# A causal pooling mixer for a prompt: band before weights, or weights before band

## What is computed

```python
u = rmsnorm(h, norm_mix[0])
for g, w in enumerate((2, 4, 8, 16)):          # 4 groups of 512 columns
    s = cs[:, P + 1:P + 1 + T, sl] - cs[:, P + 1 - w:P + 1 - w + T, sl]   # window sums of u
    cnt = jnp.minimum(pos + 1, w)
    outs.append(s / cnt)
d = pooled - u
y = einsum('btgc,gcd->btgd', d, w_group) * scale   # one 512x512 matrix per group
h = h + y
h = h + sq_relu_mlp(rmsnorm(h, norm_ffn[0]), w_up[0], w_down[0])
```

## Time and profile before

| | us |
|---|---|
| median of 3 runs | 2453.6 (2453.4 to 2454.82) |
| profiled execution, its own time | 2453.96 |
| its span, first to last instruction | 2452.2 |
| TensorE busy | 2438.4 |
| VectorE busy | 1193.2 |
| ScalarE busy | 908.8 |
| GpSimd busy | 484.9 |
| mean granted TensorE clock | 0.999 |

### The profile page before, as it was taken

The page is one execution under the profiler, slowest core; times in us unless marked ns, Lnnn a source line. Parts: engine busy times, 40 slices in busy tenths (PEclk is TensorE's granted clock), DMA queues, the critical chain, the costliest instruction groups (busy, mean ns, idle before and its releaser), DMA issues.

```text
span 2452.2 us, 43354 instructions
## 1 busy us (share of the span) xinstructions
PE 2438.4 (99%) x16326; PEld 2397.8 (98%) x16326; DVE 1193.2 (49%) x1353; ACT 908.8 (37%) x1080; POOL 484.9 (20%) x616
## 2 busy tenths in 40 slices
PE   9999999999999999999999999999999999999998
PEld 9999999999999999999888899999999999999997
DVE  6644344344444454544578885544344444434444
ACT  6332333333323333323456553332233333323332
POOL 7620022012102332210011112230022013101331
PEclk9999999999999999999999999999999999999999
DMA  6544454454444444555477764444444445445443
GB/s 234 172 151 152 147 153 147 149 150 147 152 146 145 154 147 140 150 142 154 143 249 234 233 202 153 146 146 154 147 153 147 150 143 152 153 146 151 149 147 116
DMA packets 198473, 389.05 MB, mean 159 GB/s; under 512 B 12277, under 2 KB 12533, under 8 KB 197929
## 3 DMA queue, kind: packets, MB, share of 16 engines
q1 hardware_dynamic: 197664, 385.78, 50.2%
q0 software_dynamic: 736, 2.27, 0.3%
HBM read 365.81 MB, written 22.65 MB: 158 GB/s over the span
## 4 chain that ended last, share of the span: by engine, by line
PE 96%; DVE 2%; DMA 1%; ACT 0%; issue 0%; SPq 0%; DVEq 0%; ACTq 0%
PE G L1662 30%; PE G L1664 30%; PE G L1663 30%; PE X L1936 1%; DMA gain<-in_mix_rows 1%; PE X L1899 1%; PE X L1943 0%; DVE cst L1573 0%; DMA w_raw<-in_pool_w 0%; PE G L1975 0%; PE G L1979 0%; PE G L1977 0%; PE X L1834 0%; PE X L1888 0%; DVE w_lo L1170 0%; PE X L1648 0%
## 5 line engine op out<-in xcount | busy, mean ns | idle before, releaser
L1170 DVE TENSOR_TENSOR w_lo<-w_raw,w_hi 128x1024 fp32r<-128x1024 f32 x648 | 826.5, 1277 | 1164.6 <-ACT w_hi L840 1161.1
L840 ACT ACTIVATE w_hi<-w_raw 128x1024 fp32r<-128x1024 f32 x608 | 644.6, 1061 | 1303.9 <-PE G L1664 1275.5
L1662 PE MATMUL G<-op_hi,w_hi 128*128 128x320 f32 x2816 | 875.7, 311 | 0.0
L1664 PE MATMUL G<-op_hi,w_lo 128*128 128x320 f32 x2816 | 871.0, 309 | 0.0
L1663 PE MATMUL G<-op_lo,w_hi 128*128 128x320 f32 x2816 | 870.9, 309 | 0.0
L1662 PE MATMUL G<-a_hi,w_hi 128*128 128x320 f32 x2304 | 714.5, 310 | 1.5 <-DVE hT L1289 0.8
L1663 PE MATMUL G<-a_lo,w_hi 128*128 128x320 f32 x2304 | 713.6, 310 | 0.0
L1664 PE MATMUL G<-a_hi,w_lo 128*128 128x320 f32 x2304 | 713.5, 310 | 0.0
L1662 PEld LDWEIGHTS G<-op_hi,w_hi 128*128 128x128 f32 x2816 | 528.9, 188 | 3.6 <-issue 1.6
L1663 PEld LDWEIGHTS G<-op_lo,w_hi 128*128 128x128 f32 x2816 | 529.0, 188 | 2.6 <-issue 1.0
L1664 PEld LDWEIGHTS G<-op_hi,w_lo 128*128 128x128 f32 x2816 | 528.9, 188 | 0.0
(11 more groups left out here) (282 smaller groups left out, 1015.0 us busy)
## 6 DMA issues: line engine op xcount, KB each, us to landing
w_raw<-in_ffn_w_up SPq DMA_DIRECT2D x256, 512.0 KB, 3.7
w_raw<-in_ffn_w_down SPq DMA_DIRECT2D x256, 512.0 KB, 3.7
w_raw<-in_mlstm_w_in SPq DMA_DIRECT2D x96, 512.0 KB, 3.9
w_raw<-in_mlstm_w_out SPq DMA_DIRECT2D x32, 512.0 KB, 4.5
cst<-in_state_mlstm_C SPq DMA_DIRECT2D x24, 512.0 KB, 3.9
out_C_sample<-cst SPq DMA_DIRECT2D x24, 512.0 KB, 3.2
w_raw<-in_pool_w SPq DMA_DIRECT2D x8, 512.0 KB, 11.4
w_raw<-in_state_mlstm_C SPq DMA_DIRECT2D x8, 512.0 KB, 4.2
```

The source lines that it names most:

```text
L840: act.activation(w_hi[:, c % RING], w_raw[:, c % RING], ACT.Copy).then_inc(w_hi_ok, 1)
L1170: v.tensor_tensor(w_lo[:, slot], w_raw[:, slot], w_hi[:, slot].bitcast(F32), ALU.subtract).then_inc(w_lo_ok, 1)
L1662: pe.matmul(G[:, m, 0:T], w_hi[:, slot, t, w], hi[:, k, :], start=first and t == 0, stop=False)
L1664: ins = pe.matmul(G[:, m, 0:T], w_lo[:, slot, t, w], hi[:, k, :], start=False, stop=last and t == CK - 1)
```

## The change

The order of the two products is turned round for the prompt. The group's weights are applied first, to the unnormed columns of x times the gains, with x as the stationary operand and 512 weight columns moving, so that the result is token-major; then the band, with the roots in it, mixes the tokens of the result and turns it feature-major. In detail:

- SyncE loads vectors, hT's first quarter and two weight chunks first; the sample rows and a slice of gains next; the prompt's rows later. Gains come in three pieces, and the last of them, hT's last quarter and the kept far inputs stand behind the load of chunk 5.
- ScalarE and VectorE split hT times the gain into a_hi and a_lo (`xt_hi`, `xt_lo`), without roots.
- The samples keep their order, band first: their sums go to G's fourth bank and are split into one operand of 64 hi and 64 lo columns (`pairs`), for which two products do for three. That gives hi and lo parts of y on 128 rows; `fold` adds them.
- y is copied out of PSUM: first prompt tile and samples by ScalarE (`y_first`, `y_samples`), second prompt tile by VectorE (`y_second`).
- TensorE mixes a group after the next group's weight products (`mix`); the last group's mixing stands behind the first chunk of the first FFN slab.
- Warm-up is 9 + 20 products in one piece. GpSimd draws fold ahead of the bands of groups 1 to 3, and all draws before any scaling. The squares of the sample tile come first.

```diff
-WARM = (13, 5, 8, 6)
+WARM = 20
+ROW_ORDER = (2, 0, 1)
...
+            sp.dma_start(vecs[:, :], A["vec_cols"]).then_inc(vecs_in, 16)
+            residual_load(0)
+            pool_load(0)
+            pool_load(1)
+            rows_load(2)
+            gain_load(0)
+            residual_load(1)
+            pool_load(2)
+            gain_load(1)
+            pool_load(3)
+            rows_load(0)
+            rows_load(1)
+            residual_load(2)
...
             for n in range(RING, 2 * GROUPS):
                 sp.wait_ge(w_lo_ok, n - RING + 1)
                 pool_load(n)
+                if n == RING + 1:
+                    gain_load(2)
+                    residual_load(3)
+                    sp.dma_start(far[0:NS, :], A["state_far"]).then_inc(far_in, 16)
...
             draw(0)
+            link(pool.memset(fold[:, :], 0.0))
+            for at in (0, NS):
+                pool.affine_select(out=fold[:, :], in_=fold[:, :], compare_op=ALU.not_equal, fill=1.0, base=-at,
+                                   pattern=[[-1, NS]], channel_multiplier=1).then_inc(fold_ok, 1)
+                pool.wait_ge(fold_ok, 2 if at else 1)
             for g in range(1, GROUPS):
                 draw(g)
+            for g in range(1, GROUPS):
                 rooted(g)
...
+            def xt_hi(k):
+                act.wait_ge(h_in[k // MT], 16)
+                act.activation(a_hi[:, k, 0:TP], hT[:, k, 0:TP], ACT.Copy, scale=vec(V_MIX + k)).then_inc(xt_hi_ok, 1)
+            def pair_hi(g):
+                act.wait_ge(s_sum, g + 1)
+                if g > 1:
+                    act.wait_ge(gemm, pool_used(g - 2, 1))
+                act.activation(pairs[:, g % 2, :, 0:NS], sample_part(G[:, 3]), ACT.Copy).then_inc(s_hi_ok, 1)
+            def y_first(g):
+                act.wait_ge(gemm, pool_tile(g, 0))
+                if g > 1:
+                    act.wait_ge(mixed, MT * (g - 1))
+                act.activation(ytok[:, g % 2, 0, :], G[:, 0, :], ACT.Copy).then_inc(y_act, 1)
...
+            for g in range(2, GROUPS):
+                xt_hi(MT * g)
+                xt_hi(MT * g + 1)
+                y_first(g - 1)
+                split_pool(2 * g)
+                xt_hi(MT * g + 2)
+                xt_hi(MT * g + 3)
+                y_samples(g - 1)
+                split_pool(2 * g + 1)
+                pair_hi(g)
+                op_his(g - 2)
+                squares_of(g - 2)
+            split(0, 0)
+            y_first(GROUPS - 1)
+            split(0, 1)
+            y_samples(GROUPS - 1)
+            op_his(GROUPS - 2)
+            squares_of(GROUPS - 2)
+            split(0, LEAD - 1)
+            op_his(GROUPS - 1)
+            squares_of(GROUPS - 1)
...
+            xt_lo(4)
+            xt_lo(5)
+            pair_lo(0)
+            split_pool(2)
+            y_second(0)
+            xt_lo(6)
+            xt_lo(7)
+            samples(1)
+            split_pool(3)
+            pair_lo(1)
             v.wait_ge(band_drawn, 1)
             half_square(1)
             tile_inverse(1)
+            rooted(0)
             half_square(2)
             tile_inverse(2)
+            rooted(1)
+            for g in range(2, GROUPS):
                 v.wait_ge(h_in[g], 16)
+                xt_lo(MT * g)
+                xt_lo(MT * g + 1)
+                split_pool(2 * g)
+                y_second(g - 1)
+                xt_lo(MT * g + 2)
+                xt_lo(MT * g + 3)
+                samples(g)
+                pooled(g - 2)
                 split_pool(2 * g + 1)
+                pair_lo(g)
...
+            def pool_rows(g, c, t):
+                at = (2 * g + c) % RING
+                for i in range(CK):
+                    k, first, last = 2 * c + i, c == 0 and i == 0, c == 1 and i == 1
+                    if t == 2:
+                        pe.matmul(G[:, t, :], pairs[:, g % 2, k, :], w_hi[:, at, i, :], start=first, stop=False, skip_group_check=True)
+                        ins = pe.matmul(G[:, t, :], pairs[:, g % 2, k, :], w_lo[:, at, i, :], start=False, stop=last, skip_group_check=True)
                     else:
+                        hi, lo = a_hi[:, MT * g + k, tok(t)], a_lo[:, MT * g + k, tok(t)]
+                        pe.matmul(G[:, t, :], hi, w_hi[:, at, i, :], start=first, stop=False, skip_group_check=True)
+                        pe.matmul(G[:, t, :], lo, w_hi[:, at, i, :], start=False, stop=False, skip_group_check=True)
+                        ins = pe.matmul(G[:, t, :], hi, w_lo[:, at, i, :], start=False, stop=last, skip_group_check=True)
+            def mix(g):
+                pe.wait_ge(y_act, 2 * g + 2)
+                pe.wait_ge(y_dve, g + 1)
+                pe.wait_ge(fold_ok, 2)
+                if g:
+                    pe.wait_ge(band_ok, 2 * g)
+                else:
+                    pe.wait_ge(band0_ok, 2)
+                for m in range(MT):
+                    if g:
+                        pe.wait_ge(evicted, MT * (g - 1) + m + 1)
+                    own = slice(m * P, (m + 1) * P)
+                    pe.matmul(X[m][:, 0:BT], ytok[:, g % 2, 0, own], band[:, g, B0:B1], start=True, stop=False, skip_group_check=True)
+                    pe.matmul(X[m][:, P:TP], ytok[:, g % 2, 1, own], band[:, g, B1:BS], start=False, stop=True, skip_group_check=True)
+                    pe.matmul(X[m][:, TP:T], ysam[:, g % 2, own], fold[:, :], start=False, stop=True, skip_group_check=True).then_inc(mixed, 1)
+            keep_warm(WARM)
+            for c in range(2):
+                pe.wait_ge(xt_lo_ok, 2 * c + 2)
+                pe.wait_ge(w_lo_ok, c + 1)
+                ins = pool_rows(0, c, 0)
+                if c:
+                    ins.then_inc(gemm, 1)
+                    samples(0)
+                pool_rows(0, c, 1).then_inc(gemm, 1)
+            pe.wait_ge(s_lo_ok, 1)
+            pool_rows(0, 0, 2)
+            pool_rows(0, 1, 2).then_inc(gemm, 1)
+            for g in range(1, GROUPS):
+                samples(g)
                 for c in range(2):
+                    pe.wait_ge(xt_lo_ok, MT * g + 2 * c + 2)
+                    pe.wait_ge(w_lo_ok, 2 * g + c + 1)
+                    for t in range(TT):
+                        if c == 0 and t == 1:
+                            pe.wait_ge(y_dve, g)
+                        elif c == 0:
+                            pe.wait_ge(y_act, 2 * g if t else 2 * g - 1)
+                        if t == 2:
+                            pe.wait_ge(s_lo_ok, g + 1)
+                        ins = pool_rows(g, c, t)
+                        if c or t == 2:
+                            ins.then_inc(gemm, 1)
+                mix(g - 1)
...
-                slab(s0, op_hi, op_lo, op_ready(j_op), lambda c: norm_sum(j_op) if c == 4 else None)
+                slab(s0, op_hi, op_lo, op_ready(j_op),
+                     lambda c: norm_sum(j_op) if c == 4 else mix(GROUPS - 1) if c == 0 and s0 == S_FFN0 else None)
```

More of the change, by code:

```diff
@@ L677, in _ @@
                 select(seqmask[at:at + NS, 2, 1:], [[TS, NSEQ]], -1, base=TS - 1)
-            link(pool.memset(fold[:, :], 0.0))
-            for at in (0, NS):
-                select(fold[:, :], [[-1, NS]], 1, base=-at, op=ALU.not_equal, fill=1.0)
             with nc.allow_non_contiguous_dma("a few values"):
@@ L911, in _ @@
+            act.wait_ge(vecs_in, 16)
+            xt_hi(0)
+            xt_hi(1)
+            split_pool(0)
+            xt_hi(2)
+            xt_hi(3)
+            split_pool(1)
             square(0)
             tile_root(0)
+            xt_hi(4)
+            xt_hi(5)
+            pair_hi(0)
+            split_pool(2)
+            y_first(0)
+            xt_hi(6)
+            xt_hi(7)
+            split_pool(3)
+            y_samples(0)
+            pair_hi(1)
             square(1)
@@ L1290, in pooled @@
                                            op0=ALU.mult, op1=ALU.add).then_inc(evicted, 1)
[L1292 to L1303 removed]
+            v.wait_ge(consts, 1)
@@ L1304, in _ @@
+            op_split(0, 0, V_FFN)
+            split(0, 0)
             op_split(0, 1, V_FFN)
-            pooled(GROUPS - 1)
+            y_second(GROUPS - 1)
+            split(0, 1)
             op_split(0, 2, V_FFN)
             op_split(0, 3, V_FFN)
-            split(0, 1)
+            pooled(GROUPS - 2)
+            op_split(0, 4, V_FFN)
+            op_split(0, 5, V_FFN)
+            pooled(GROUPS - 1)
             split(0, LEAD - 1)
-            for k in (4, 5):
-                op_split(0, k, V_FFN)
@@ L1701, in samples @@
+                pe.wait_ge(u_ok, g + 1)
+                if g:
+                    pe.wait_ge(s_lo_ok, g)
+                if g == GROUPS - 1:
+                    pe.wait_ge(far_in, 16)
                 for i in range(MT):
-                    at = slice(TP + i * NS, TP + (i + 1) * NS)
-                    ins = pe.matmul(X[0][:, at], xrow[0:rows, 2, features(g, i)], band[0:rows, g, BS:BP], start=False,
```

(32 more changed lines are left out.)

249 lines of the change are left out of this document (107 added, 142 removed).

## The result

The changed kernel takes 2461.73 us (median of 7; 2460.15 to 2464.11) against 2453.4 of the kernel before beside it: ratio 1.0034, 95% interval 1.0024 to 1.0043, slower by 8.3 us. The forecast was 2456.5, with a range of 2452 to 2461. The profiled execution took 2463.59, with a span of 2461.8 against 2452.2.

What follows compares the result with a forecast made beforehand. TensorE's instruction stream was taken to bound the kernel. The old median 2453.6, plus 1.3 us for a later second FFN chunk and 1.6 for a low-clock spell, gave 2456.5 us, range 2452 to 2461.

Steps and rivals of the forecast that it cites:

- the third wait of TensorE: Idle ahead of the last group's sample products, samples(3), at 44.2 us; put at 0.2 us.
- the clock: One spell at the lower level of 1.2 GHz near 47 to 50 us, costing 1.6 us as before.
- the work behind the mark: TensorE's stream after the second FFN chunk's start; no added waits, the tightest point being chunk 3 at 70.9.
- The stream of products: TensorE's first stage without waits: start, weights, samples, mixing, first FFN chunk and re-starts, 61.0 us in sum.
- warm-up and not data sets the start: First weight product at 10.4 us, when warm-up ends; its operands' splits end at 9.1.
- the mark: Moment TensorE enters the second FFN chunk: 62.54 before, 63.8 forecast; a microsecond there is one in the total.
- the second wait: Idle of TensorE ahead of samples(2), behind VectorE's splits and copy; put at 1.0 us.
- The waits of TensorE in the stage: Idles ahead of samples(1), (2) and (3) in the first stage: 1.6, 1.0 and 0.2, together 2.8 us.
- the slower rival: Twice the waits before the samples and three more clock spells, as element engines' order binds; 2462.5 us, chance 0.20.
- At full clock I had 2454.9: Rival in which the clock holds through the new order; with waits gone too 2452.1; chance 0.27 for both.
- a cover of 1.1 us: Slack at FFN chunk 3, needed at 70.9: VectorE's operand splits done by 69.8.
- wait 1: Idle of TensorE ahead of samples(1), whose VectorE chain restarts only with the sample sums; put at 1.6 us.

Runs made afterwards that it cites:

- run 9: 14 in place of 20 warm-up products behind the first 9, against the kernel of run 8; 2458.47 us, ratio 1.0016.
- run 12: Changed kernel with all repairs and moved normalisations, plus 14 warm-up products, two normalisations left in the slab, FFN chunk 2 split earlier; 2453.76 us, ratio 0.9999.
- run 1: Changed kernel with GpSimd's sums of squares held back until the last sample columns are normalised; 2458.86 us, ratio 1.0018.
- run 3: Changed kernel with 6 identity products ahead of samples(1) and 8 ahead of samples(3) on TensorE, filling the idle; 2459.09 us, ratio 1.0022.
- run 6: Changed kernel with ScalarE's squares of the last four tiles moved behind the split of FFN chunk 3; 2461.74 us, ratio 1.0033.
- run 8: Changed kernel with the edits of run 2, run 4 and run 6, and VectorE's pair split ahead of chunk split and evictions; 2456.89 us, ratio 1.0015.
- run 7: Changed kernel with VectorE's four normalisations of kept prompt columns moved ahead of the first FFN split; 2461.07 us, ratio 1.0028.
- run 2: Changed kernel with VectorE's samples(1) ahead of chunk 2's split and samples(2), samples(3) at the head of their group; 2458.27 us, ratio 1.0016.
- run 11: Repaired kernel with moved normalisations, the last group's sample products set between the two chunks of group 2; 2458.87 us, ratio 1.0017 to the kernel before.
- run 4: Changed kernel with the last group's sample products in two runs, four near then four far, not in turn; 2459.36 us, ratio 1.0024.
- run 5: The kernel before, with the last group's sample products in two runs, four near then four far; 2452.29 us, ratio 0.9995.

## Why the prediction was wrong

Three terms failed: the third wait of TensorE (0.2 us put down, 1.81 measured), the clock (one stretch and 1.6 us put down; two and 5.9 in the profiled execution, about 3 in the median), and the work behind the mark, which I had at nothing (1.8 us of waits). The stream of products was right.

*The stream of products: right.* Weight products 0.233 each less re-starts (group 2: 32 in 7.55 us), a mixing 2.7, samples 0.9, FFN chunk 3.6, start 9.93 for 10.4. That warm-up and not data sets the start held by a little only: the chunk split ended at 9.33 where I had 9.1, and with six warm-up products less (runs 9 and 12) TensorE waited for it until 9.8. With both low stretches taken out (1.5 in group 1, 9.09 against 7.55; 2.0 in the last samples, 4.91 against the 2.87 of run 1; 2.4 in group 3, 9.90 against 7.55; 5.9 in all), the mark stands at 64.1 where the sum had 63.8. Run 3, at full clock, has it at 64.95, since the second wait is then there.

*The waits of TensorE in the stage: total nearly right (2.8; 3.5 measured), the third mis-sized.* First 1.54 for 1.6. The second 0.1 for 1.0, because the low clock made TensorE late itself; with full clock in group 1 it was 0.8 (runs 1 and 3). So at full clock the total would be near 4.2, and that it looked nearly right is partly luck. The third 1.81 for 0.2: I priced VectorE's steps from rows without GpSimd's sums beside them, 1.9 us too little over four steps (shown by run 1). I had even seen that GpSimd's scalings end near 39, and asked only who waits for them, not what follows them. The Trainium skill has the rule ("SBUF — State Buffer", SBUF: two separate sides): a VectorE instruction with two SBUF inputs and a GpSimd one that reads SBUF exclude each other. The trace agrees: chunk split, column split and sample columns, all of two SBUF inputs, were stretched, and the copy from PSUM was not. The kernel before shows the other side of it, beside the same adds:

```profile
39.68 1.22 DVE L1170 TENSOR_TENSOR w_lo<-w_raw,w_hi 128x1024 fp32r<-128x1024 f32 x1
39.69 1.94 POOL L657 TENSOR_TENSOR acc<-acc,junk 128x320 f32<-128x320 f32 x1
```

Here the split started first and kept its 1.22, and the add took 1.94 where one alone takes 0.88. The operand split behind it (40.81) took 1.17 us where one alone takes 0.54, so the slowing could be read from the old trace.

*The clock: the largest miss in the profiled execution, not in the median.* I took one stretch, 1.6 us, as before. The profiled execution had two, one of them three times as long, 5.9 us. I wrote that idles beside small products may bring it down, and gave this to the slower rival at 0.20. Runs 1 and 3 show the chain: slowed VectorE, idle of 1.8, low clock; filling the idle kept the clock full. In the profiled execution the fall came as the samples began, so they took 4.9 instead of 2.9 us; in run 6, behind the same idle, it came after them. The median lies 1.9 below the profiled execution, and by run 3 the low clock cost it about 3 us, 1.4 more than I had put down. At full clock I had 2454.9, and run 3 took 2459.09: the greater part of the miss in the median lies in waits, of the stage and behind the mark.

*Behind the mark: failed.* I gave chunk 3 a cover of 1.1 us and the rest none. It waited 1.03, since ScalarE split its weights only at 74.09, behind the last squares (run 6 moved these and the wait went), and since VectorE's split and operand splits then took 1.95 and 1.61 us beside GpSimd's sums:

```profile
73.25 4.59 POOL L685 TENSOR_TENSOR acc<-acc,junk 128x320 f32<-128x320 f32 x4 [2.19 <-ACT junk L965]
75.17 1.95 DVE L1241 TENSOR_TENSOR w_lo<-w_raw,w_hi 128x1024 fp32r<-128x1024 f32 x1 [3.03 <-ACT w_hi L865]
```

And I never walked VectorE's list to the end of the first slab, where TensorE waited 0.80. "A microsecond at the mark is one in the total" was false in both directions: runs 6 and 8 show that a lead there is lost again, as VectorE then has 2.96 us of work for each 3.52 of TensorE and a reciprocal and two splits before it may evict.

*The ledger.* Mark 70.00 for 62.54: 7.5. The two waits behind it cost more than their 1.8 us of idle, as TensorE starts anew after each: from its last product ahead (77.00 and 96.40) to the next (78.34 and 97.51), less one spacing of 0.15, 1.2 and 1.0 us. Together 9.6, all of what lies between the profiled executions.

*The rival.* The slower one was what happened, at 2462.5 for 2461.73 (2463.59 profiled), though its waits were not doubled: in the profiled execution the clock did more and VectorE's list behind the mark the rest. That the two numbers are so near is luck. Given 0.20, it should have had most of the chance, since wait 1 and the far samples both stood in my own walk.

*Open.* Which executions fall to the lower clock, and for how long. Over all profiles, with near and far products in turn a stretch came beside the last samples or behind them in five of seven (both kernels, runs 1, 6 and 7; not in runs 2 and 3); with them apart in one of seven (run 11, behind an idle of 2.19). An idle of 1.5 us ahead of samples(1) was followed by a stretch in two profiles (the changed kernel, run 6) and not in three (runs 1, 4 and 7). So spacing and idle both seem to bear on it, and neither decides it alone. How much of the 8.3 us is clock comes out alike in two ways, both estimates: run 3 gives about 3 us; and the profiled execution with full clock, its second wait back at 0.8, would take 2463.6 - 5.9 + 0.8 = 2458.5, which is 5.1 above the kernel before and leaves 3.2.

## What to carry to other kernels

A head start in a stage ends at the next gate of another engine: walk every engine's list to the first point behind the change where it has slack again, not only to the point where the old stream begins. Price each step of a helper engine with its neighbour at work, when both read SBUF. And where TensorE's stretch of small fp32 products meets a wait, remove the wait or fill it: in the profiled execution the low clock cost more (5.9 us) than the waits of the stage (3.5).

## What the runs showed of the hardware

Alternating stationary operands of 120 and 64 rows spaces the records of 64-column fp32 products by 0.18 us, against 0.12 to 0.13 in runs of one kind (run 4: 2.04 us for 16; run 5: 1.96). A copy out of PSUM was not slowed by GpSimd's adds (0.68); a split of two SBUF inputs was, from 1.21 to 1.86, where an add was under way as it started, and in the kernel before, where the split started first, it kept 1.22 and the add took 1.94. The start behind the same 58 warm-up records stood between 9.85 (run 6) and 11.12 us (run 7): in run 6's profile 11 records a us began from 5.0 on, in run 7's only from 8.0, and 7 or 8 a us until then, though both list a granted clock of 1.00 there.
